# Prompt attention: the causal mask of the turned scores as a product on VectorE instead of a matmul on TensorE

## The reference, cut to what matters

```python
m_s = (kpos <= qp[None, None, :, None, None])            # selected branch: causal
s_s = jnp.einsum('bqgrd,bqgksd->bqgrks', qr_b, kb) * scale
p_s = masked_softmax(s_s, m_s)
o_s = jnp.einsum('bqgrks,bqgksd->bqgrd', p_s, vb)
...
m_w = (wpos >= 0) & (wpos <= qp) & (wpos > qp - WINDOW)  # window of 512: causal
p_w = masked_softmax(s_w, m_w)
o_w = jnp.einsum('bqgrk,bkgd->bqgrd', p_w, vw_b)
return g_b[..., 0:1] * o_c + g_b[..., 1:2] * o_s + g_b[..., 2:3] * o_w
```

## Time and profile before

| what | value |
|---|---|
| median of three runs | 1624.1 us (1623.59 to 1624.1) |
| the profiled execution, its own time | 1627.97 us |
| span of that execution | 1625.7 us |
| PE busy | 1567.8 us, 96% of the span |
| DVE busy | 945.9 us, 58% |
| ACT busy | 738.8 us, 45% |
| POOL busy | 186.7 us, 11% |

### The profile page before, as it was taken

How to read it: one execution, slowest core, us unless ns; L and a number is a source line. 1 busy time by engine, 2 the same in 40 slices (tenths; PEclk the granted TensorE clock), 3 DMA queues, 4 the chain that set the end, 5 groups by cost and what they waited for, 6 DMA issues and landing times.

```text
span 1625.7 us, 31499 instructions
## 1 busy us (share of the span) xinstructions
PE 1567.8 (96%) x13500; PEld 1448.7 (89%) x13500; DVE 945.9 (58%) x1227; ACT 738.8 (45%) x1283; POOL 186.7 (11%) x194
## 2 busy tenths in 40 slices
PE   8999899999999999999999879999999999999998
PEld 7788598999999999999999655565999999999998
DVE  6898547667383746633342565663376755647472
ACT  5434565436162544432232457665454352616342
POOL 1000000002020110010240352210000020202000
PEclk9999999999999999999999989999999999999999
DMA  7543143222223141321236400001313232222321
GB/s 204 143 120 95 43 147 120 91 84 96 82 92 117 62 169 64 104 85 54 77 105 213 131 1 1 1 1 58 99 53 104 79 117 92 96 74 93 116 78 56
DMA packets 139767, 146.96 MB, mean 90 GB/s; under 512 B 6578, under 2 KB 131330, under 8 KB 139295
## 3 DMA queue, kind: packets, MB, share of 16 engines
q1 hardware_dynamic: 138351, 138.23, 27.2%
q0 software_dynamic: 1280, 6.75, 1.3%
HBM read 132.08 MB, written 10.87 MB: 88 GB/s over the span
## 4 chain that ended last, share of the span: by engine, by line
PE 86%; DVE 7%; ACT 4%; issue 2%; DMA 1%; SPq 1%; ACTq 0%; DVEq 0%
PE ps L408 46%; PE ps L801 5%; PE ps L800 5%; PE ps L799 5%; PE ps L541 3%; PE ps L1627 2%; PE ps L1474 2%; PE ps L1473 2%; PE ps L1475 2%; PE ps L2154 2%; PE ps L2132 2%; DVE w_lo L393 1%; PE ps L2075 1%; PE ps L2133 1%; PE ps L594 1%
## 5 line engine op out<-in xcount | busy, mean ns | idle before, releaser
L408 PE MATMUL ps<-hid_hi,w_hi 128*128 128x272 f32 x1280 | 268.9, 289 | 2.2 <-DVE hid_lo L2455 1.5
L408 PE MATMUL ps<-hid_hi,w_lo 128*128 128x272 f32 x1280 | 267.3, 288 | 0.0
L408 PE MATMUL ps<-hid_lo,w_hi 128*128 128x272 f32 x1280 | 266.7, 288 | 0.0
L393 DVE TENSOR_TENSOR w_lo<-w_raw,w_hi 128x2048 fp32r<-128x2048 f32 x71 | 165.0, 2324 | 122.3 <-ACT w_hi L388 120.4
L388 ACT ACTIVATE w_hi<-w_raw 128x2048 fp32r<-128x2048 f32 x71 | 135.4, 1907 | 174.9 <-PE ps L408 171.7
L408 PE MATMUL ps<-x_hi,w_hi 128*128 128x272 f32 x896 | 201.6, 292 | 11.3 <-DVE x_lo L2994 4.3
L408 PEld LDWEIGHTS ps<-hid_hi,w_hi 128*128 128x128 f32 x1280 | 201.9, 188 | 3.9 <-issue 2.3
L408 PEld LDWEIGHTS ps<-hid_lo,w_hi 128*128 128x128 f32 x1280 | 202.2, 189 | 0.0
L408 PEld LDWEIGHTS ps<-hid_hi,w_lo 128*128 128x128 f32 x1280 | 201.0, 189 | 0.0
L408 PE MATMUL ps<-x_hi,w_lo 128*128 128x272 f32 x896 | 198.9, 289 | 0.0
L408 PE MATMUL ps<-x_lo,w_hi 128*128 128x272 f32 x896 | 198.3, 288 | 0.0
(11 more groups left out here) (438 smaller groups left out, 3260.8 us busy)
## 6 DMA issues: line engine op xcount, KB each, us to landing
w_raw<-in_ffn_w_out SPq DMA_DIRECT2D x64, 512.0 KB, 4.4
w_raw<-in_ffn_w_in SPq DMA_DIRECT2D x58, 512.0 KB, 3.8
w_raw<-in_nsa_w_in SPq DMA_DIRECT2D x20, 512.0 KB, 4.5
w_raw<-in_ple_w_gate SPq DMA_DIRECT2D x16, 512.0 KB, 3.9
w_raw<-in_conv_w_in SPq DMA_DIRECT2D x15, 512.0 KB, 6.1
w_raw<-in_conv_w_out SPq DMA_DIRECT2D x8, 512.0 KB, 4.0
w_raw<-in_nsa_w_o SPq DMA_DIRECT2D x8, 512.0 KB, 4.6
conv_in_turned<-conv_in SPq DMA_DIRECT2D x16, 203.2 KB, 2.6
```

The lines of the kernel that those rows point to most:

```text
L393: dve.tensor_tensor(WL[par][:, :], RAW[par][:, :], WH[par][:, :].bitcast(F32), ALU.subtract)\
L408: m = pe.matmul(o_, w[par][:, wcols:wcols + P], x[:, k, c_], start=f, stop=l)
```

## The change

The mask matmuls of `turned` are taken away. ACT's exponential is taken of unmasked scores, and a new DVE step, `masked`, sets the masked places in the diagonal blocks to zero, in place: it takes the smaller of the value and 3e38 and multiplies by a tile of ones and zeros (M01, made once at the start of DVE's `rest`). `values(i)` waits for the mask of unit i on DVE instead of for the exponential on ACT. `turned` still waits for the exponential alone. `scores` keeps its mask matmuls.

```diff
+        (M01,), e = over(p_at + 6656, ("causal_ones", [P, P], F32))
...
+        S["t_masked"] = S["pe_full"]
...
                     pe.matmul(out, ka[:, br, k], qa[:, who, kt * P:SEQ], start=first, stop=False)
-                    pe.matmul(out, kb[:, br, k], qb[:, who, kt * P:SEQ], start=False, stop=False)
-                    masks.append((out[:, 0:P] if t < 4 else out[:, :, 0:P], mask))
-                for x, (out, mask) in enumerate(masks):
-                    m = pe.matmul(out, CAUB[:, :], mask, start=False, stop=t < 5 or x == 1)
+                    m = pe.matmul(out, kb[:, br, k], qb[:, who, kt * P:SEQ], start=False, stop=t < 5 or x == 1)
                 m.then_inc(S["t_full"], 1)
...
-                pe.wait_ge(S["t_exp"], i + 1)
+                pe.wait_ge(S["t_masked"], 1 + i + 1)
...
+            def masked(i):
+                t = i % 6
+                dve.wait_ge(S["t_exp"], i + 1)
+                if t < 4:
+                    b = PT[:, i % 2, :, 0:P]
+                elif t == 4:
+                    b = PT[:, i % 2, :, :].rearrange("p b (h n) -> p (b h) n", h=2)[:, :, 0:P]
+                else:
+                    b = PT[:, i % 2, 0, :].rearrange("p (b n) -> p b n", b=4)
+                ones = M01[:, :].rearrange("p (o n) -> p o n", o=1).broadcast_to([P, 2 if t < 4 else 4, P])
+                L(dve.scalar_tensor_tensor(b, b, 3e38, ones, ALU.min, ALU.mult), S["t_masked"], wait=False)
...
             def rest():
                 L.count[S["k_ready"]] = 2
+                L(dve.scalar_tensor_tensor(M01[:, :], CST[:, C_CAU:C_CAU + P], 0.0, ID, ALU.is_lt, ALU.add), wait=False)
...
                     if p + LEAD < N_S:
                         maxima(p + LEAD)
+                    masked(p)
                     if p:
                         for hd in m_slot(p):
                             rows(hd)
```

More of the change, by code:

```diff
@@ L2120, in turned @@
                 qa, qb, ka, kb = QA[c % 3], QB[c % 3], KA[c // 2 % 2], KB[c // 2 % 2]
-                idb = IDB[:, :].rearrange("p (o n) -> p o n", o=1).broadcast_to([P, 2, P])
                 kt = t // 2 if t < 4 else t - 2
                 k, n = slice(kt * P, (kt + 1) * P), SEQ - kt * P
-                masks = []
                 for x in range(2):
                     if t < 4:
-                        out, br, who, mask, first = PS[:, 4 + x, 0:n], t % 2, x, IDB[:, :], True
+                        out, br, who, first = PS[:, 4 + x, 0:n], t % 2, x, True
                     else:
@@ L2130, in turned @@
                         out = out.rearrange("p (h n) -> p h n", h=2)
-                        br, who, mask, first = x, slice(0, 2), idb, t == 4 or x == 0
+                        br, who, first = x, slice(0, 2), t == 4 or x == 0
                     pe.matmul(out, ka[:, br, k], qa[:, who, kt * P:SEQ], start=first, stop=False)
-                    pe.matmul(out, kb[:, br, k], qb[:, who, kt * P:SEQ], start=False, stop=False)
-                    masks.append((out[:, 0:P] if t < 4 else out[:, :, 0:P], mask))
-                for x, (out, mask) in enumerate(masks):
-                    m = pe.matmul(out, CAUB[:, :], mask, start=False, stop=t < 5 or x == 1)
+                    m = pe.matmul(out, kb[:, br, k], qb[:, who, kt * P:SEQ], start=False, stop=t < 5 or x == 1)
                 m.then_inc(S["t_full"], 1)
```

## The result

The changed kernel takes 1639.6 us (median of five runs, 1637.5 to 1644.1) against 1624.1 for the kernel before on the same chip (1623.6 to 1629.1): a ratio of 1.0082, 95% interval 1.0064 to 1.0099, or +13.3 us (10.4 to 16.1). It is slower, as forecast; the forecast of +9.0 was too small. The median lies 1.1 us above the upper end of the range; by the ratio, for which all runs of both kernels count, the time is 1637.4, inside it.

The account below looks back on a forecast made before the run. PE, busy 96% of the span, was taken to bound the kernel, with a DVE end in every chunk but the last. Chunks +6.75, POOL 2.0 and ones-tile 0.2 gave +9.0 us, median 1633.1; range 1625 to 1638.5.

Parts of the forecast that it names:

- the ones-tile: Making the ones-tile on DVE between POOL's instructions, ahead of unit 0: 0.2 us added.
- the plain sum: Prompt attention stage, all eight chunks' changes added up without waits for POOL: +6.75 us.
- The place: At a chunk's end, what stands behind a mask in DVE's queue counts; both long masks lie there, despite 74 us idle.
- PE's saving: 96 mask matmuls removed in the stage: 0.70 us a chunk, 5.6 us, back only where PE sets the pace.
- Prices of the masks: On DVE, 0.45 us for a short mask (t below 4), 0.72 for a long one; the stage 26 us.
- The half-rate rival: DVE masks run at half rate, 7.4 us more over seven chunk ends, 1640.5 us; chance 0.04.
- Chunks 2 and 4: At their ends the mask of unit 16 waits for its exponential, with shift and cmp_shift behind it: +2.1 us each.
- Chunk 0: Mask 1 holds back shift and cmp_scale, savings of units 0 to 3 lost, two long masks at the end: +1.1 us.
- the sum by chunks: Each chunk's change against its own start, added over the stage without POOL or a clock fall: +6.75 us.
- Chunks 1, 3, 5, 6 and 7: Plain ends of 1, 5, 6: +0.2, +0.6, +0.2 us; chunk 3 with the weight slab +0.9; chunk 7 -0.45.
- POOL: Masks 5, 11, 17, 23 and 29 at ends of chunks 0 to 4 wait 0.4 us each: 2.0, bounds 0 and 6.4.
- The clock: Rival: PE's clock falls in idle gaps at ends of chunks 2 and 4, about 2 us each, 1637; chance 0.12.

Follow-up runs that it names:

- the last version: Against the kernel before: short masks on DVE behind rows, shift and cmp_shift, t = 5 on DVE behind q_row, t = 4 still PE mask matmuls; 1626.8 us, ratio 0.9984.

## Why the prediction was right or wrong, point by point

The stage's +14.6 us split by the runs, in the order in which they take things away: 5.3 from the clock, 4.1 that come back when POOL is moved from the ends, 5.5 in chunks 0 to 5 of what is left, less 0.3 in chunks 6 and 7. The forecast had 0, 2.0, 7.0 and -0.25, and 0.2 for the ones-tile, which lies ahead of the stage, where no run can tell it from the 8 us over which unit 0 began. The 5.5 still hold what POOL costs in its new place. Counted the other way, DVE's instructions at the ends of chunks 0 to 4 of after were 5.8 us longer beside POOL than the shortest of their kind; if all of it was lost, as the run with POOL later shows for chunks 2 and 4 (1.93 and 1.59 us longer, 1.91 and 1.58 lost), POOL is 5.8 and the plain sum 3.7, an estimate. Either way the plain sum was too large and POOL too small. Without the clock the stage would be 9.3 us longer, where the forecast had 8.75 for it: that is luck, since the two errors cancel.

- **The place.** Right: the chunk's end decides, and DVE's mean of idle time says nothing. 13.4 us of short masks cost 1.2, and moving all masks behind `shift` and q_row gave 14.7 back.
- **PE's saving.** Right in size (5.6 forecast, 5.3 seen without masks), and right that most of it does not arrive; 0.3 us in chunks 6 and 7 and what chunk 0 saves do.
- **Prices of the masks.** Right: 0.42 and 0.69 against 0.45 and 0.72. The half-rate rival fell. The rule of the Trainium skill behind it (Vector Engine (DVE) Microarchitecture Reference, section Points that are easy to get wrong) does not agree with the trace: 512 elements of two fp32 SBUF operands took 0.69 us, what the product of the earlier trace rows takes.
- **Chunks 2 and 4.** The mechanism was right to the instruction, the wait of 1.20 us among it; +2.1 each was 1.45 and 1.83 with POOL moved and the clock up.
- **Chunk 0** was the worst term of the sum by chunks: +1.1 against +0.13 with POOL moved. Counting the savings of units 0 to 3 as lost was the step that failed. Maxima 12, in before and then in after, 17.78 and 17.18 us behind unit 0:

```profile
979.25 1.23 DVE L2261 TENSOR_REDUCE neg_max<-ps 128x2 f32<-128x1024 f32 x1 [2.62 <-PE ps L2079]
```

```profile
973.82 1.23 DVE L2258 TENSOR_REDUCE neg_max<-ps 128x2 f32<-128x1024 f32 x1 [2.37 <-PE ps L2081]
```

So 0.60 us of savings did arrive there, and the end behind it grew by 0.72 (6.27 to 6.99, POOL moved), not 1.1.

- **Chunks 1, 3, 5, 6 and 7.** Chunks 1, 5 and 6 with 7 were within 0.3. Chunk 3 is +1.36 against +0.9, but with POOL beside its first units; with POOL at its end, less the 0.90 us that it holds DVE up there, it is +0.4, an estimate. So whether that term was too cheap or too dear isn't shown.
- **POOL.** The term was mis-sized, 2.0 against 4.1, or 5.8 by the other count (both within its bounds), because I put it on the wrong instructions. I read the earlier trace rows as two instructions with two SBUF operands each, and so charged the masks; the five lost 0.22 each, 1.1 in all. The cast and the tensor-scalar, with one operand, lost 0.4 to 1.0, the cast even beside a memset, which has no input in its row. No semaphore stands between them and POOL, so these engines do not meet at semaphores alone. Masks can lose more, where they fall on POOL's subtraction: 1.74 us instead of 0.69 with the masks behind (at 1050.56). The section of the Trainium skill that I had cited (SBUF — State Buffer, section SBUF: two separate sides) names that case too, a DVE instruction in a two-port mode against any GpSimd one; I had weighed only its other half. The trace agrees with it: 0.89 beside the memset, 0.17 without; which mode the cast ran in no run shows.
- **The clock.** The step that failed most: the sum put it at nothing. It stood among the rivals at 0.12, with some 2 us for each of two places; it fell in three places for 5.3 us, at the end of chunk 0 too, where the +1.1 of the sum on top of the old 0.31 makes a gap of about 1.4 us (1.38 with POOL moved, without a fall), and POOL made it 2.00. The price was near (1.42, 2.48 and 1.44), though ten us at 0.68 would lose 3.2 with PE busy all along. It should not have stood against the forecast but in it: the sum itself said that PE would stand idle for 3 us, and behind all three waits for q_row of 2.99 us and more in the stages of these runs the clock fell (behind those of 1.99 to 2.76, in three cases of five).

The profile showed what the prediction named: units 18 and 30 wait 3.34 and 2.99 us for q_row, DVE rows follow each other there, and the mask of unit 16 waits for ACT. No mask was over 1 us, as some should have been; the longest is 0.90.

## What to carry to other kernels

Before work is moved to an engine with idle time, list what stands behind it in that engine's queue at the place where the other engines wait; there the same 26 us cost 20 us in one order, clock and POOL included, and 5 in another. When a sum says that PE will stand idle for microseconds, add what PE then loses to its clock. And a busy engine's gain may need only half of a change: what is free goes over, what stands at the waiting place stays.

## What the runs showed of the hardware

- The granted clock fell behind waits of PE of 1.99, 2.00, 2.13, 2.99, 3.05 and 3.34 us, and stayed at 1.00 behind 2.13 and 2.76 elsewhere. With the masks behind, it fell once behind 1.64 and 0.49 us. In chunk 7 the same two waits (1.3 and 0.68 us) came with a fall in two runs and without one in after and in three other runs. What decides between them stays open.
- A fall cost 1.4 to 2.5 us here; useless matmuls in the waits (6, 11 and 10) kept the clock at 1.00 behind them and gave that back.
- DVE instructions with one SBUF operand and 8 or 16 elements a partition can wait up to 1 us for POOL (0.99 in after), for its memset too (0.72). A mask, with two operands, waited up to 1.1 us (1.78 at 1000.46 in the last version). A tensor-reduce over 128 x 512 kept its 0.69 us beside POOL's casts (1025.21 in after).
